# A two-block transformer kernel on one core: x and weight loads interleaved, first three outputs by part and block, memory sums one output later

## What is computed

```
hn = rmsnorm(x, attn_norm_g[0])        # x: 512 tokens x 1024
proj = hn @ w_in                       # c_q 384 | c_kv 256 | k_r 32 | q_cross 256 columns
kv = (rmsnorm(c_kv, kv_norm_g) @ w_ukv)
q  = (rmsnorm(c_q, q_norm_g) @ w_uq)
mem_n = rmsnorm(mem, mem_norm_g)       # mem: 256 tokens x 1024
kv_mem = mem_n @ w_mem_kv
```

## Time and profile before

| | us |
|---|---|
| median of the 3 runs shown | 1880.42 (1880.04 to 1880.89) |
| the profiled execution | 1880.36 |
| its span (first to last instruction) | 1878.6 |
| TensorE busy in it | 1862.0 |
| VectorE, ScalarE, GpSimd busy | 862.3, 791.5, 1015.1 |

### The profile page before, as it was taken

How to read it: one execution, slowest core, us unless ns; L and a number is a source line. 1 busy time by engine, 2 the same in 40 slices (tenths; PEclk the granted TensorE clock), 3 DMA queues, 4 the chain that set the end, 5 groups by cost and what they waited for, 6 DMA issues and landing times.

```text
span 1878.6 us, 26672 instructions
## 1 busy us (share of the span) xinstructions
PE 1862.0 (99%) x9075; PEld 1552.6 (83%) x9075; DVE 862.3 (46%) x1744; ACT 791.5 (42%) x1416; POOL 1015.1 (54%) x1340
## 2 busy tenths in 40 slices
PE   8999999999999999999999999999999999999999
PEld 6878888888888888888888888887878888888887
DVE  6777542222236675422222673697752354444200
ACT  6558642323233576432232353647642333233221
POOL 6750465455556654655555564455565456555553
PEclk9999999999999999999999999999999999999999
DMA  6330132332322212332323323221022322332332
GB/s 213 124 107 1 42 100 101 98 95 99 100 91 90 85 40 69 107 100 91 101 91 99 101 79 98 71 75 38 24 95 96 101 90 91 101 99 89 112 101 79
DMA packets 47437, 168.29 MB, mean 90 GB/s; under 512 B 5616, under 2 KB 5872, under 8 KB 47088
## 3 DMA queue, kind: packets, MB, share of 16 engines
q1 hardware_dynamic: 46368, 164.64, 27.2%
q10 hardware_dynamic: 976, 2.39, 0.4%
HBM read 164.13 MB, written 2.10 MB: 88 GB/s over the span
## 4 chain that ended last, share of the span: by engine, by line
PE 93%; DVE 4%; ACT 2%; issue 1%; DMA 0%; POOL 0%; SPq 0%; DVEq 0%; ACTq 0%
PE bank L677 27%; PE bank L679 27%; PE bank L678 27%; PE bank L762 3%; PE bank L808 3%; PE bank L799 2%; PE bank L780 1%; DVE ACC L1483 1%; PE bank L775 0%; ACT WH L1072 0%; DMA X<-x 0%; PE bank L970 0%; PE bank L720 0%; DVE ML_ L1738 0%; DVE XL L1764 0%
## 5 line engine op out<-in xcount | busy, mean ns | idle before, releaser
L588 POOL TENSOR_TENSOR WL<-RAW,WH 128x256 fp32r<-128x256 f32 x1208 | 936.2, 806 | 702.9 <-ACT WH L1072 702.6
L677 PE MATMUL bank<-XH,WH 128*128 128x512 f32 x1311 | 521.4, 398 | 0.8 <-POOL WL L588 0.2
L679 PE MATMUL bank<-XH,WL 128*128 128x512 f32 x1311 | 510.8, 390 | 0.0
L678 PE MATMUL bank<-XL,WH 128*128 128x512 f32 x1311 | 510.6, 389 | 0.0
L1072 ACT ACTIVATE WH<-RAW 128x1024 fp32r<-128x1024 f32 x302 | 316.7, 1051 | 301.3 <-PE bank L679 296.5
L679 PEld LDWEIGHTS bank<-XH,WL 128*128 128x128 f32 x1311 | 246.1, 188 | 51.9
L677 PEld LDWEIGHTS bank<-XH,WH 128*128 128x128 f32 x1311 | 246.3, 188 | 49.6 <-issue 0.7
L678 PEld LDWEIGHTS bank<-XL,WH 128*128 128x128 f32 x1311 | 246.5, 188 | 47.6 <-issue 0.7
L677 PE MATMUL bank<-HH,WH 128*128 128x512 f32 x512 | 199.2, 389 | 0.0
L679 PE MATMUL bank<-HH,WL 128*128 128x512 f32 x512 | 199.2, 389 | 0.0
L678 PE MATMUL bank<-HL,WH 128*128 128x512 f32 x512 | 199.2, 389 | 0.0
(11 more groups left out here) (381 smaller groups left out, 2816.8 us busy)
## 6 DMA issues: line engine op xcount, KB each, us to landing
RAW<-stream SPq DMA_DIRECT2D x302, 512.0 KB, 3.4
out<-X SPq DMA_DIRECT2D x8, 256.0 KB, 4.5
X<-x SPq DMA_DIRECT2D x3, 512.0 KB, 8.3
MEM<-mem SPq DMA_DIRECT2D x1, 1024.0 KB, 11.0
W<-cmp_w ACTq DMA_DIRECT2D x1, 1024.0 KB, 4.6
KT<-KR ACTq DMA_DIRECT2D x1, 768.0 KB, 8.9
CT<-consts SPq DMA_DIRECT2D x1, 513.0 KB, 12.2
X<-x SPq DMA_DIRECT2D x2, 256.0 KB, 3.3
```

Source lines behind the costliest of these rows:

```text
L588: ins = pool.tensor_tensor(WL[:, slot, c], RAW[:, slot, c], WH[:, slot, c].bitcast(F32), ALU.subtract)
L677: pe.matmul(dst, lhs[0], rhs[0], start=start, stop=False)
L678: pe.matmul(dst, lhs[0], rhs[1], start=False, stop=False)
L679: return pe.matmul(dst, lhs[1], rhs[0], start=False, stop=stop)
```

## The change

The queue now issues weight tiles 0 and 1 behind the second piece of x and tile 2 behind the third; tile 3 is issued ahead of the memory instead of behind it. TensorE's warm-up has six matmuls instead of three. `first_outputs` no longer takes output by output: it takes blocks of x (h, the high part, and l, the low part) for one or two outputs at a time in the list `arrival`, and from block 4 on each part for all three outputs. Its sum of the squares of x stands behind the third output's low weights instead of the second's. The sums for the memory move from behind output 4 to behind output 5, and the spreading of the memory's scale from behind output 5 to behind output 6, ahead of the sums for c_kv, which stay behind output 6. ScalarE converts tiles 0 and 1 behind block 1, tile 2 behind block 3, and tile 3 behind the second square.

```diff
--- before.py
+++ after.py
@@ -557,14 +557,12 @@
             sp.dma_start(GV[:, 0:KD], gains[:, 0:KD]).then_inc(signal("first_gains_in"), 16)
             for first, n in X_PIECES:
                 sp.dma_start(X[:, first:first + n, :], x[:, first:first + n, :]).then_inc(x_in[first], 16)
-                if first == 1:
-                    load(0, 0, stream[0])
-            load(1, 1, stream[1])
+                for n in {1: (0, 1), 2: (2,)}.get(first, ()):
+                    load(n, n, stream[n])
             sp.dma_start(CT[:, 0:CONST_LATE], consts[:, 0:CONST_LATE]).then_inc(consts_in, 16)
             sp.dma_start(GV[:, KD:], gains[:, KD:]).then_inc(consts_in, 16)
-            load(2, 2, stream[2])
+            load(3, 3, stream[3])
             sp.dma_start(MEM[:], mem).then_inc(mem_in, 16)
-            load(3, 3, stream[3])
             sp.dma_start(POSB0[:], pos_rows[0]).then_inc(signal("pos_in"), 16)
             sp.dma_start(POSI[:], pos_cols).then_inc(signal("pos_in"), 16)
             sp.dma_start(CT[:, CONST_LATE:], consts[:, CONST_LATE:]).then_inc(signal("late_consts_in"), 16)
@@ -837,21 +835,27 @@
 
             def warm_up():
                 pe.wait_ge(signal("acc_set"), 1)
-                for _ in range(3):
+                for _ in range(6):
                     ins = pe.matmul(BANK[7][:], ACC[:, 0:P], ACC[:], start=True, stop=True)
                 ins.then_inc(signal("acc_read"), 1)
 
             def first_outputs(n, after):
 
                 steps = [plan.steps["in0"][j * KD:(j + 1) * KD] for j in range(n)]
-                for j in range(n):
-                    pe.wait_ge(hi_done, j + 1)
-                    for t, c, width, k, o, _, _, _ in steps[j]:
-                        for a, part in ((XH, "in0_x_hi"), (XL, "in0_x_lo")):
+                first_blocks = ("h0", "l0", "h1", "l1")
+                arrival = [((0,), first_blocks), ((1,), first_blocks), ((0, 1), ("h2", "h3", "l2")),
+                           ((2,), first_blocks + ("h2", "h3")), ((0, 1), ("l3",)), ((2,), ("l2", "l3"))]
+                arrival += [(range(n), [part + str(k)]) for k in range(NT, KD) for part in "hl"]
+                for outs, parts in arrival:
+                    for part in parts:
+                        a, ready, k = (XH, "in0_x_hi", int(part[1])) if part[0] == "h" else (XL, "in0_x_lo", int(part[1]))
+                        for j in outs:
+                            if part == "h0":
+                                pe.wait_ge(hi_done, j + 1)
                             if j == 0:
-                                pe.wait_ge(signal(part), k + 1)
-                            pe.matmul(BANK[o % RING][:], WH[:, t % RING, c:c + width], a[:, k, :],
-                                      start=k == 0 and part == "in0_x_hi", stop=False)
+                                pe.wait_ge(signal(ready), k + 1)
+                            t, c, width, _, o, _, _, _ = steps[j][k]
+                            pe.matmul(BANK[o % RING][:], WH[:, t % RING, c:c + width], a[:, k, :], start=part == "h0", stop=False)
                 for j in range(n):
                     pe.wait_ge(lo_done, j + 1)
                     for t, c, width, k, o, _, _, _ in steps[j]:
@@ -862,10 +866,9 @@
                         after[j]()
 
             warm_up()
-            first_outputs(3, {1: sums("in0")})
+            first_outputs(3, {2: sums("in0")})
             dense(lambda _: plan.steps["in0"][3 * KD:], 0, operand(XH, XL), o0=plan.out0["in0"],
-                  after={3: [scales("in0")], 4: [sums("mem", NMEM)], 5: [scales("mem", NMEM, RMEM)],
-                         6: [sums("c_kv")]})
+                  after={3: [scales("in0")], 5: [sums("mem", NMEM)], 6: [scales("mem", NMEM, RMEM), sums("c_kv")]})
 
             def rotate_key():
                 pe.wait_ge(signal("late_consts_in"), 16)
@@ -1213,12 +1216,13 @@
                     act.wait_ge(x_in[m], 16)
                 x_hi("in0", "attn0", m)
                 if m == 1:
-                    keep_ahead(in0, 0)
-            keep_ahead(in0, 1)
+                    keep_ahead(in0, 1)
+                elif m == 3:
+                    keep_ahead(in0, 2)
             for m in range(KD):
                 square("in0", m, X[:, m, :])
-                if m == 3:
-                    keep_ahead(in0, 2)
+                if m == 1:
+                    keep_ahead(in0, 3)
             keep_ahead(in0)
             act.wait_ge(mem_in, 16)
             act.wait_ge(consts_in, 32)
```

## The result

The changed kernel takes 1886.15 us, median of 7 runs (1884.09 to 1886.54); the kernel before, with four more runs than were shown, 1878.85 us (1878.57 to 1880.89). The ratio is 1.0034, 95% interval 1.0024 to 1.0044, so 6.4 us slower with 4.5 to 8.3 as bounds (the two medians by themselves are 7.3 apart). The profiled execution took 1885.78, its span 1884.0: 5.4 more than before. The lines of after carry other numbers: L718 is L720 of before (sums), L675 to L677 are L677 to L679, L858 and L862 are L853 and L858, L586 is L588, L1075 is L1072, and L1487 (additions) is L1483.

A forecast was written before the change was run, and what follows sets the result against it. TensorE's matmul queue was taken as the bound, with VectorE equally late at the c_kv and c_q sums. Front 0, memory sums +5.44, chain -0.44 and clock +2.1 made +7.1 on 1880.36: 1887.5 us, range 1883.0 to 1889.5.

The forecast's parts named there:

- Rival 1: Whole kernel slower by the same cause, but the clock stays up or the chain covers it: +5.0, 1885.4; chance 0.12.
- Rival 2: Front transfers land as before whatever the order, x blocks aren't late, the front keeps 1.6: 1885.8; chance 0.10.
- front, at output 4: Up to output 4's start: lead used up waiting for tile 4, so 0 gained, bounds -1.6 to +1.0 us.
- memory sums a place later: Memory sums behind output 5 instead of output 4 come 24 matmuls later: +5.44 us, near 47.6.
- from them to the c_kv sums: VectorE's chain from memory sums to c_kv sums takes 11.85 for 12.29: -0.44 us, bounds -1.3 to +0.2.
- clock, and what the chain covers: Behind the wait at the c_kv sums, 4.8 us at the lower clock: +2.1 us, bounds 0 to +2.4.
- The wait: TensorE waits 5 to 6 us ahead of the c_kv sums near 59.5; VectorE idles 3 us before the memory sums.
- Rival 3: Front later still: TensorE also loses the clock at the sums of x and output 4: 1889.5; chance 0.06.
- rival 4: No measurable change: angle operations run alone at half their time, front keeps 1.6, no clock lost: 1880; chance 0.12.
- Rival 5: Faster: TensorE alone sets the pace, output 3 starts 3.7 earlier, gain 4.5: 1875.9; chance 0.05.

The follow-up runs named there:

- the filled wait: Changed kernel plus 22 unread matmuls on TensorE ahead of the c_kv sums: 1883.09 us, ratio 1.0018 to the kernel before.
- memory sums put back: Changed kernel with the memory sums behind output 4 and the spreading of the memory's scale behind output 5 again: 1879.64 us, ratio 0.9999.
- memory sums inside output 5: Changed kernel with the memory sums behind output 5's second block, spreading and c_kv sums as in the kernel before: 1880.88 us, ratio 1.0009.
- later c_q sums: Kernel with memory sums inside output 5, plus the c_q sums behind output 4 of stage mem instead of output 3: 1881.74 us, ratio 1.0010.
- memory wait filled: Kernel with memory sums put back, plus seven unread matmuls ahead of the memory sums: 1880.74 us, ratio 1.0004.
- c_kv squares first: Changed kernel, VectorE's c_kv additions ahead of the angle operations, ScalarE's c_kv squares ahead of converting tiles 8 and 9: 1885.16 us, ratio 1.0030.
- scale of c_kv ahead: Kernel with memory sums inside output 5, later c_q sums, c_kv squares first, plus VectorE's c_kv scale before the second angle group: 1879.69 us, ratio 1.0001.

## Why the prediction was right

The time forecast was 1887.5, 7.1 above the profiled execution of before; measured were 1886.15 as the median and 5.4 between the profiled executions, ratio 6.4. The direction, the place and the mechanism held. The time alone would not have shown that: rivals 1 and 2, at 1885.4 and 1885.8, fit it as well as the forecast does, and only the profile and the experiments tell them apart. Term by term, read at the c_q sums:

| term | forecast | measured |
|---|---|---|
| front, at output 4 | 0 | 35.25 - 36.61 = -1.36 |
| memory sums a place later | +5.44 | 4.09 + 1.36 = +5.45 |
| from them to the c_kv sums | 11.85 - 12.29 = -0.44 | 11.45 - 12.29 = -0.84 |
| clock, and what the chain covers | +2.1 | 22.39 - 20.01 = +2.38 |
| sum at the c_q sums | +7.1 | +5.63 |

- Front: too pessimistic by 1.4, inside its bound of -1.6. This is the largest error of the sum. The transfers came in the order and at the pace forecast (tile 1 converted at 10.22, the last x blocks' low parts over at 19.2 for 19.3) and the additions ended at 27.8 for 28.1. The mis-sized step is the low part of the memory: I took 0.51 an operation from five operations beside the end of GpSimd's work; without GpSimd eight take 3.25, 0.41 each (the line at 27.69). The scale of x came at 30.86 for 32.2, tile 4 in time for 35.25 for 36.6, and TensorE waited 0.3 there and not 1.5.
- Memory sums: as forecast, since 24 matmuls at full clock were the whole of it.
- The chain behind them: 0.4 too long. I had only the first of the nine angle operations alone; the second was too, since GpSimd started behind it in the kernel after:

```profile
48.30 7.62 POOL L586 TENSOR_TENSOR WL<-RAW,WH 128x256 fp32r<-128x256 f32 x8 [2.47 <-ACT WH L1075]
```

- The wait: 5.13 at 57.71, forecast 5 to 6 near 59.5; VectorE idle 3.80, forecast 3.
- The clock: the lower level lasted from about 56.9 to 63.7 and TensorE worked 6.0 us in it, not 4.8; half of that is 3.0, of which 0.6 was covered, and 2.4 was left, not 2.1. Rival 1, by which it would be free, fell with the filled wait: with the clock kept at 1.00 the c_q sums come 2.3 earlier.
- Rival 2 fell with the landings, though the lead that it kept at the front (1.6) is nearly what came of it (1.36), for another reason. Rival 3 fell with a granted clock of 1.00 from 25 to 37 us, rival 4 with tensor-scalar angle operations at 0.83 to 0.97 where 0.43 is their time alone. Rival 5 was the right question to ask: TensorE at full clock, with the six warm-up matmuls in either kernel, gained nothing (ratios 1.0001 and 1.0030, the latter for three in place of six). The Trainium skill, TensorE: Matmul & The Clock Gate, section "Loop structure matters more than you think", has a wait for a DMA between matmuls as what makes TensorE cold. The rows agree: behind the wait of 4.19 for the first tile the granted clock was 0.50. They also say that behind it VectorE was the one to wait for, and so the warmth was worth nothing here.

The front's bound of -1.6 was the better value than the 0 I took, and the range of 1883.0 to 1889.5 had it in. The range's upper end was added up with 0.2 for the chain and 2.8 for the clock, where the bounds stated in the sum are 0.64 above the 5.0 (+0.2 for -0.44) and 2.4; the two slips cancel to 0.1. The spans differ by 5.4 and the ratio says 6.4; its interval has both, and nothing here settles the rest.

## What to carry to other kernels

Moving a small step later on the busy engine is free for that engine and not for those that wait for it: follow the step's result, list what stands behind the waiting instruction on its engine, and see when the busy engine wants that. Here a reduction of 0.4 us moved by 24 matmuls held VectorE for 3.8 us and came back as a wait of 5.1. When two engines are even at a later point, a lead of one at the front is worth nothing by itself: six kernels that tried to keep 1.4 us of it gained nothing that the times show. And a wait can cost more than its length: behind the one of 5.1 the lower clock cost another 2.3 us. Behind the one of 1.5 (memory sums put back) it cost 0.5 at the c_q sums and nothing in the time, since VectorE was as late there.

## What the runs showed of the hardware

TensorE can lose its clock behind idle times much shorter than the 4.2 us of the earlier trace rows. The granted clock fell behind waits of 1.52 us (memory sums put back), 1.91 us (memory sums inside output 5) and 1.94 us (the same with later c_q sums), and at the start of two kernels, behind the warm-up, behind waits of 1.52 and 1.74 us (later c_q sums; memory wait filled). In each case it fell only 1.1 to 1.7 us after TensorE had started again, and stayed down for about 3.4 us. Waits of 1.12 (start of the changed kernel), 1.15 (c_kv squares first) and 1.27 (scale of c_kv ahead) did not lose it. Seven matmuls that nobody reads, in the place of the 1.5 us, kept it at 1.00. The Trainium skill, TensorE: Matmul & The Clock Gate, section "Loop structure matters more than you think", has an idle time of 8 us in its example of a TensorE gone cold; the shortest that did it here is 1.52.

ScalarE began to convert the first weight tile, right behind its landing, between 7.1 and 9.0 us in the profiles of these kernels, although the transfers ahead of it are the same in all of them. The span moves with it: the changed kernel with three warm-up matmuls has 1882.6 with a first conversion at 7.24, the changed kernel 1884.0 with one at 8.97, and their distances to the c_q sums are 71.35 and 71.13. So a comparison of two profiles to 1 us should count from that conversion.

VectorE beside GpSimd: a tensor-scalar operation on 512 columns from SBUF took 0.43 alone and 0.83 to 0.97 beside GpSimd's subtraction, one with two inputs from SBUF (L1577 to L1579 of the changed kernel) 0.69 alone and 1.09 to 1.11 beside it, a copy of 512 columns out of a PSUM bank 0.69 in either case (at 42.38 above, GpSimd idle, and 0.68 at 69.89 in the kernel with the scale of c_kv ahead, GpSimd busy throughout). The Trainium skill, GPSIMD Engine Reference, section "1. Specifications", has GpSimd's SBUF interfaces shared with VectorE and contention for instructions in a 2-port mode or with two SBUF inputs. The operations with two inputs agree, and so does the copy from PSUM, which kept its time. Whether the tensor-scalar operations ran in a 2-port mode no run here shows.
